# Silu and sigmoid of the last mixer written with tanh of half the argument, one gate tile a step

## The reference

```python
u = xn @ w_in[i]
(a_b, a_c, a_h, a_z, n_q, n_kc, n_vc, n_ks, n_vs, n_kw, n_vw, n_g, n_z,
 d_q, d_k, d_v, d_z) = jnp.split(u, split_points, axis=-1)
y_a = a_b * _short_conv(a_c * a_h, conv_w[i], conv_b[i]) * jax.nn.silu(a_z)
gates = jax.nn.sigmoid(n_g)
y_b = _nsa(n_q, ..., gates, ...) * jax.nn.silu(n_z)        # its compression: silu(flat @ w1) @ w2
y_c = _dilated_mixer(d_q, d_k, d_v) * jax.nn.silu(d_z)     # groups weighted by softmax of their lse
h = h + jnp.concatenate([y_a, y_b, y_c], axis=-1) @ w_out[i]
```

## Time and profile before

| | |
|---|---|
| median of 3 runs | 1572.01 us (1570.42 to 1573.85) |
| profiled execution, its own time | 1571.54 us |
| its span, first to last instruction | 1569.8 us |
| mean granted TensorE clock | 0.975 |
| TensorE busy | 1474.7 us, 94% of the span |
| VectorE busy | 781.5 us, 50% |
| ScalarE busy | 613.3 us, 39% |
| GpSimd busy | 567.2 us, 36% |
| the last mixer's loop | from about 1150 us to 1467 us of the span |

### The profile page before, as it was taken

One profiled execution on the slowest core, in us unless ns is written; L12 is line 12 of the kernel. 1 busy time (PEld: TensorE's weight loads), 2 busy tenths in 40 slices (PEclk: granted clock), 3 DMA queues, 4 the chain that ended last, 5 costly groups with the idle time before them and its releaser, 6 DMA issues.

```text
span 1569.8 us, 20390 instructions
## 1 busy us (share of the span) xinstructions
PE 1474.7 (94%) x7122; PEld 1153.0 (73%) x7122; DVE 781.5 (50%) x1405; ACT 613.3 (39%) x1110; POOL 567.2 (36%) x236
## 2 busy tenths in 40 slices
PE   6988999999999998889999999999988899899997
PEld 5656778888888886456778888888866677666785
DVE  6774442223444688784442223444655246566434
ACT  5443332332223436664442232322433244564431
POOL 3322254444444344111354444444334442122341
PEclk9999999999999999989999999999989999999998
DMA  5211233322233232100232223322222322111221
GB/s 210 78 53 56 73 102 96 102 96 94 94 102 98 68 108 81 41 28 28 68 107 94 94 94 103 98 94 94 81 71 91 107 90 73 41 55 48 74 68 54
DMA packets 36624, 129.55 MB, mean 83 GB/s; under 512 B 4048, under 2 KB 4176, under 8 KB 36560
## 3 DMA queue, kind: packets, MB, share of 16 engines
q1 hardware_dynamic: 35136, 124.80, 24.2%
q10 hardware_dynamic: 1424, 3.90, 0.7%
HBM read 126.58 MB, written 2.10 MB: 82 GB/s over the span
## 4 chain that ended last, share of the span: by engine, by line
issue 57%; POOL 22%; PE 17%; DVE 2%; ACT 1%; POOLq 1%; DVEq 0%; ACTq 0%
POOL w L623 22%; PE bank L640 4%; PE bank L642 4%; PE bank L641 4%; PE bank L765 1%; PE bank L779 1%; PE bank L745 1%; DVE arena L2149 0%; POOLq L622 0%; POOLq L620 0%; ACT tmp L1238 0%; DVE arena L1775 0%; DVE arena L2039 0%; ACT tmp L1228 0%; ACT arena L1519 0%
## 5 line engine op out<-in xcount | busy, mean ns | idle before, releaser
L623 POOL TENSOR_TENSOR w<-raw,w 128x1024 fp32r<-128x1024 f32 x232 | 567.0, 2447 | 968.6 <-ACT w L1180 598.4
L640 PE MATMUL bank<-opC,w 128*128 128x512 f32 x624 | 256.8, 411 | 26.4 <-POOL w L623 14.7
L642 PE MATMUL bank<-opC,w 128*128 128x512 f32 x624 | 247.2, 396 | 0.0
L641 PE MATMUL bank<-opC,w 128*128 128x512 f32 x624 | 246.9, 396 | 0.0
L1751 DVE TENSOR_TENSOR mlp_op<-arena,mlp_op 128x512 fp32r<-128x512 f32 x64 | 144.5, 2260 | 188.7 <-ACT mlp_op L1295 188.7
L1267 ACT ACTIVATE w<-raw 128x1024 fp32r<-128x1024 f32 x126 | 133.2, 1057 | 239.5 <-PE bank L642 239.5
L640 PE MATMUL bank<-mlp_op,w 128*128 128x512 f32 x544 | 212.7, 391 | 6.7 <-DVE arena L1663 6.0
L641 PE MATMUL bank<-mlp_op,w 128*128 128x512 f32 x544 | 212.2, 390 | 0.0
L642 PE MATMUL bank<-mlp_op,w 128*128 128x512 f32 x544 | 212.1, 390 | 0.0
L640 PE MATMUL bank<-opA,w 128*128 128x512 f32 x416 | 163.4, 393 | 5.5 <-DVE opA L1589 2.2
L642 PE MATMUL bank<-opA,w 128*128 128x512 f32 x416 | 162.0, 389 | 0.0
(11 more groups left out here) (215 smaller groups left out, 1934.7 us busy)
## 6 DMA issues: line engine op xcount, KB each, us to landing
raw<-stream_dram SPq DMA_DIRECT2D x232, 512.0 KB, 3.4
out_t_dram<-arena SPq DMA_DIRECT2D x8, 256.0 KB, 2.2
x<-x_t_dram SPq DMA_DIRECT2D x4, 256.0 KB, 5.6
x<-x_t_dram ACTq DMA_DIRECT2D x4, 256.0 KB, 7.1
rope<-ropes_dram ACTq DMA_DIRECT2D x2, 512.0 KB, 6.8
con<-consts_dram ACTq DMA_DIRECT2D x1, 993.5 KB, 8.0
arena<-p_t_dram ACTq DMA_DIRECT2D x1, 512.0 KB, 4.1
par<-params_dram ACTq DMA_DIRECT2D x1, 253.5 KB, 3.8
```

The source lines that it names most:

```text
L623: pool.tensor_tensor(w_lo[:, j, :], raw[:, j, :], w_hi[:, j, :].bitcast(F32), ALU.subtract).then_inc(lo_made, 1)
L640: pe.matmul(out, wh, hi, start=first, stop=False)
L641: pe.matmul(out, wh, lo, start=False, stop=False)
L642: return pe.matmul(out, wl, hi, start=False, stop=last)
```

## The change

Silu(x) is written as x (1 + tanh(x/2)) / 2 and sigmoid(x) as (1 + tanh(x/2)) / 2. ScalarE computes tanh with scale 0.5 into one of five spare buffers (two of `rope`, two of `more`, one of `rms`), for one gate tile a step, in the step after the tile came out of PSUM. VectorE then makes (tanh + 1) times the tile, in place, with one scalar_tensor_tensor (`gate_of`, L2118), at the head of `behind_last` of that step. A new semaphore, `silu_done`, counts these products; from the sixth tile on, ScalarE waits for it before it reuses a buffer. The factor 1/2 is moved: into the sparse gates (the eviction multiplies by 0.25), into the logarithm of the dilated groups (scale 2.0), into the compressed keys and values (times 0.5 at eviction), into the last product of the convolution.

```diff
+        SILU = (18, 19, 20, 30, 31, 32, 6, 7)
+        half_tanh = [rope[:, 0, :], rope[:, 1, :], more[:, 2, :], more[:, 3, :], rms[:, 2, :]]
...
                 if name == "hid1":
                     act.wait_ge(z_ready, z_tile("hid1") + 1)
-                    nc.scalar.activation(z2(17)[0:32, :], z2(17)[0:32, :], ACT.Sigmoid).then_inc(silu_made, 1)
+                    nc.scalar.activation(z2(17)[0:32, :], z2(17)[0:32, :], ACT.Tanh, scale=0.5).then_inc(silu_made, 1)
                     for i in range(2):
-                        nc.scalar.activation(hid[:, 2 + i, :], hid[:, i, :], ACT.Sigmoid).then_inc(hid_sig, 1)
+                        nc.scalar.activation(hid[:, 2 + i, :], hid[:, i, :], ACT.Tanh, scale=0.5).then_inc(hid_sig, 1)
...
-                    nc.scalar.activation(z2(29), z2(28), ACT.Ln).then_inc(lse_exp, 1)
+                    nc.scalar.activation(z2(29), z2(28), ACT.Ln, scale=2.0).then_inc(lse_exp, 1)
                     act.wait_ge(lse_exp, 4)
                     nc.scalar.activation(z2(29), z2(29), ACT.Exp, scale=-1.0).then_inc(lse_exp, 1)
-                for i in {32: (18, 19, 20, 30, 31, 32), 7: (6, 7)}.get(name, ()):
-                    act.wait_ge(z_ready, z_tile(i) + 1)
-                    nc.scalar.activation(z2(i), z2(i), ACT.Silu).then_inc(silu_made, 1)
+                if name in SILU:
+                    n = SILU.index(name)
+                    act.wait_ge(z_ready, z_tile(name) + 1)
+                    if n >= len(half_tanh):
+                        act.wait_ge(silu_done, n - len(half_tanh) + 1)
+                    nc.scalar.activation(half_tanh[n % len(half_tanh)], z2(name), ACT.Tanh, scale=0.5).then_inc(silu_made, 1)
...
                 if name == "gates":
-                    step(nc.vector.tensor_copy(gates[:, :], src[:, 0:TT * 32]))
+                    step(TS(gates[:, :], src[:, 0:TT * 32], 1.0, 0.25, ALU.add, ALU.mult))
                     TS(gates[:, 0:18:3], gates[:, 0:18:3], c("late"), None, ALU.mult).then_inc(z_ready, 1)
                 elif name == "cmp":
-                    mark(nc.vector.tensor_copy(cmpk[:, :], src[:, 0:32]))
-                    nc.vector.tensor_copy(cmpv[:, :], src[0:32, P:2 * P]).then_inc(z_ready, 1)
+                    mark(TS(cmpk[:, :], src[:, 0:32], 0.5, None, ALU.mult))
+                    TS(cmpv[:, :], src[0:32, P:2 * P], 0.5, None, ALU.mult).then_inc(z_ready, 1)
...
-                        TTn(hid[:, kv, :], hid[:, kv, :], hid[:, 2 + kv, :], ALU.mult).then_inc(hid_made, 1)
+                        STT(hid[:, kv, :], hid[:, 2 + kv, :], 1.0, hid[:, kv, :], ALU.add, ALU.mult).then_inc(hid_made, 1)
...
                 if name == 6:
-                    dve.wait_ge(silu_made, 7)
+                    dve.wait_ge(silu_done, 6)
...
-                        dve.wait_ge(silu_made, 8 + j)
+                        dve.wait_ge(silu_done, 7 + j)
                         step(TTn(z2(4 + j), z2(4 + j), z2(j), ALU.mult))
-                        TTn(z2(4 + j), z2(4 + j), z2(6 + j), ALU.mult).then_inc(src_ready, 1)
+                        STT(z2(4 + j), z2(4 + j), 0.5, z2(6 + j), ALU.mult, ALU.mult).then_inc(src_ready, 1)
...
-                    dve.wait_ge(silu_made, 4)
+                    dve.wait_ge(silu_done, 3)
                     TTn(z2(15 + k), src[:, :], z2(15 + k), ALU.mult).then_inc(o_out, 1)
 
+            def gate_of(name):
+
+                n = SILU.index(name)
+                dve.wait_ge(silu_made, n + 2)
+                STT(z2(name), half_tanh[n % len(half_tanh)], 1.0, z2(name), ALU.add, ALU.mult).then_inc(silu_done, 1)
+
             def behind_last(s):
+                for name in Z_DONE[s - 1] if s else ():
+                    if name in SILU:
+                        gate_of(name)
                 for name in Z_DONE[s]:
                     evict(name)
                     after_evict(name)
```

More of the change, by code:

```diff
@@ L415, in program @@
         gates_turned, gates_ready = sem("gates_turned"), sem("gates_ready")
+        silu_done = sem("silu_done")
         log_den, lse_ready, lse_full, lse_exp = sem("log_den"), sem("lse_ready"), sem("lse_full"), sem("lse_exp")
```

## The result

The changed kernel takes 1560.43 us (median of 4 runs, 1559.53 to 1561.90) against 1571.22 us for the kernel before on the same chip. Of the 4.0 us between the forecast time (1564.4) and the measured one, 0.8 is the median of the kernel before, which was 1572.01 when the forecast was made. Measured twice more, the changed kernel had 1561.22 and 1561.20 us. In the first of these two one execution of six took 1569.95 us, with a granted clock of 0.972 where the others have 0.978 to 0.981; it has no profile, and its cause is open.

A forecast was written before the change was run, and what follows sets the result against it. TensorE, busy for 94% of the span, was taken as the bound. Terms 5.2 + 2.0 + 0.7 - 0.3 = 7.6 us off 1571.54 gave 1563.9, plus 0.5 for the median: 1564.4 us; range 1561.8 to 1568.8 us.

The forecast's parts named there:

- The gap, 5.2 us: TensorE's 7.33 us gap at 1346.54 us: one tanh replaces load, six silus, load; gap falls to 2.1 us, 5.2 us gained.
- The clock behind it, 2.0 us: Stretch right behind the gap at 1346.54 us: the granted clock holds after a 2.1 us gap, 2.0 us gained, bounds 0 and 2.0.
- the first rival: Behind the shortened gap the granted clock falls all the same: 2.0 us stay lost, gain 5.6 us, 1566.4 us; chance 0.30.
- Tiles 6 and 7, 0.7 us: TensorE's 0.68 us gap at 1383.25 us goes, as both table loads go and one activation moves a step earlier: 0.7 us.
- Sigmoids and the six early tanhs, 0: Sigmoids at 1264 us and tanhs moved to earlier steps: hidden behind TensorE's filling, 0; bound 0.1 to 0.3 us for the tanhs.
- The products, -0.3 us: Eight new VectorE products, mostly in idle time; not wholly hidden at tiles 18 and 6: 0.3 us lost, bounds 0 and 0.6.
- The sum: All terms together: 5.2 + 2.0 + 0.7 - 0.3 = 7.6 us gained, forecast 1564.4 us.
- more comes back: Low clock of 1446 to 1450 us doesn't occur either, 1.5 us more gained: 1562.9 us; chance 0.10.
- The range: Predicted time of the whole kernel: 1561.8 to 1568.8 us, widened below by 1.0 us for the scatter of a median.
- the products were not held up by GpSimd: Rival: GpSimd's pieces hold VectorE's new products to 2.8 us each: 1570.6 or 1586.5 us; chance 0.12 partly, 0.03 slower.
- tanh came without a load: Rival on ScalarE: tanh not in the exponentials' table, so each brings two loads, 2.57 us a step; given no chance.

The follow-up runs named there:

- the last edit: Changed kernel with the convolution's products moved behind other steps and its two-operand work spread clear of GpSimd's piece: 1556.98 us, ratio to the kernel before 0.9906.

## Why the prediction was wrong

The direction was right, and so were the place and the mechanism of the terms that it has; the gain was 3.2 us too small, because the sum left out what the change does to the clock of the code behind it. By the steps of the prediction:

- **The gap, 5.2 us.** Measured 5.44 (7.33 to 1.89, forecast 2.1). Right. The five other lengths (4.48, 4.73, 4.53, 3.21, 7.84 us) follow ScalarE's work ahead of the copy each time.
- **The clock behind it, 2.0 us, "with doubt".** Measured 2.04, and the clock held behind the gap of 1.89 us in all eight profiles that have it, and behind 3.21 us in one, but not behind 4.48 and 4.53. The number was right, but what it was chosen by doesn't hold, and so far it was luck. It rested on the gap of 2.21 us at 45 us with the full clock behind it; in nine of the 20 profiles the same gap has the low clock behind it. Behind the gap of 2.49 us at 1205 us, on which the first rival stood, the clock is low in all 20, though at this place it holds behind 3.21 us. The length of a gap alone doesn't decide.
- **Tiles 6 and 7, 0.7 us.** Measured 0.77. Right.
- **Sigmoids and the six early tanhs, 0.** Right: 1560.92 us with the sigmoids kept, and no new gap in the profile.
- **The products, -0.3 us.** 0: leaving them out or doubling them changed no gap. The idle time behind a product was a fair bound; that a delay of VectorE by 0.3 us doesn't reach TensorE while ScalarE has a step of lead is the likely reason, but isn't tested by itself.
- **The sum.** This is the step that failed. It ended behind the mixer's last edited tile, as if the clock of the later code were given: the low stretch of 1446 us and the norm stood in it at nothing, without a reason. The case "more comes back" named the low stretch of 1446 to 1450 us and priced it right (1.5 us, measured 1.5), but I gave it 0.10. It occurred in three profiles out of three of the changed kernel. And nobody had priced the same thing in the last norm, whose sums took 1.87 us at the low clock and 1.05 at the full one; with the matmuls after them 1.2 us. Together 2.7 us of 10.95, and of the 3.2 us that the forecast lacks; the rest is the products (0.3) and the gap (0.2).
- **The range.** Its lower end was the case "more comes back" (1562.9) less 1.0 us of scatter, put down as 1561.8. With the norm's term it would have been 1560.6, at the edge of the result.

Rival by rival: the clock did not fall all the same; the products were not held up by GpSimd, though that mechanism is in this kernel and held up a tap by 2.0 us in an experiment; tanh came without a load.

What stays open: why the low stretches prefer some kernels. Shown is that they stand behind the short gaps of 1395 to 1447 us, that they are missing in the profiles without these gaps (one of the kernel before, one of the changed kernel with the last edit), that they come and go between executions of one kernel, and that the one profile with 1.3 us more of delay ahead of them has one again. That the shift of 8 us is what rid the changed kernel of them is one reading, and not shown; no run moved the code by 8 us without changing a gap. It can't be the time from the start of the program alone: the changed kernel's third profile passes the same matmuls 2.0 us earlier than its first and has no low stretch either. The same holds for the norm.

## What to carry to other kernels

An activation batch that is longer than the consumer's lead should be spread over the steps, but only with functions of the loop's own table: spreading alone opened new gaps of 1.8 us, changing tables alone left the clock low right behind the gap, and the two together gave more than the sum. A gap that goes has a second price behind it, in the clock, and a third one further on, where short gaps and a lowered clock meet: give the case "low clocks behind the edit go too" a real share of the chance. Before an instruction with two SBUF operands is moved on VectorE, look at what GpSimd does at its new place; the convolution's products moved away gave some 1.2 us with the collision and 4.2 without.

## What the runs showed of the hardware

- A table load cost its 1.28 us and little more: two of them shortened a gap by 2.85 us.
- The granted clock held behind TensorE gaps of 1.89 us (eight profiles) and 3.21 us (one) at this place and was low behind 4.48, 4.53, 4.73, 7.33 and 7.84 us. Elsewhere in the same program it was low behind 2.49 us in all 20 profiles, behind 2.2 us at 45 us in nine of them, and behind 1.22 and 0.40 us in the changed kernel but not in the kernel before.
- Low stretches of one kernel differ between executions: none and two, 3.1 us, with the same instructions and the same gaps of 0.56 to 1.38 us. A single profile that shows such a stretch doesn't tell that the kernel always pays for it.
- A scalar_tensor_tensor of 0.75 us took 2.8 us beside a GpSimd piece of 2.52 us, and a tensor_scalar from SBUF was held up beside another such piece; reductions from PSUM with one SBUF operand were not.
